# Eight-kilobyte weight runs, and an activation turn moved one step later, in an expert loop on one core

## The reference, cut to what matters

```python
g = jnp.einsum('td,edf->tef', h, p['w_gate'])      # w_gate (64, 1024, 256)
u = jnp.einsum('td,edf->tef', h, p['w_up'])        # w_up   (64, 1024, 256)
a = jax.nn.silu(g) * u * comb[..., None].astype(h.dtype)
routed = jnp.einsum('tef,efd->td', a, p['w_down']) # w_down (64, 256, 1024)
```

## Time and profile before

| | us |
|---|---|
| median of 3 runs | 1307.94 |
| lowest and highest | 1305.64, 1310.03 |
| span of the profiled execution, first to last instruction | 1303.8 |
| PE, DVE, ACT, POOL busy | 1130.0, 391.3, 324.9, 306.5 |
| first gate/up product of an item starts | 567.14 |
| last one starts | 1204.92 |

### The profile page before, as it was taken

How to read it: one execution, slowest core, us unless ns; L and a number is a source line. 1 busy time by engine, 2 the same in 40 slices (tenths; PEclk the granted TensorE clock), 3 DMA queues, 4 the chain that set the end, 5 groups by cost and what they waited for, 6 DMA issues and landing times.

```text
span 1303.8 us, 19553 instructions
## 1 busy us (share of the span) xinstructions
PE 1130.0 (87%) x6570; PEld 656.3 (50%) x6571; DVE 391.3 (30%) x936; ACT 324.9 (25%) x708; POOL 306.5 (24%) x500
## 2 busy tenths in 40 slices
PE   3899999898999897489998698899999889988960
PEld 1676676465666544354554344455554445544630
DVE  2200000284553223622222122222222212222587
ACT  2000100295663111222222222222222212222111
POOL 1000100102222000333333233333333323333123
PEclk9699999998997898689999999999999989999995
DMA  9711321213440005729899999999999999899651
GB/s 320 278 65 65 109 93 65 74 64 130 165 159 1 1 1 186 274 88 351 310 350 372 369 374 369 369 366 314 322 340 363 369 362 371 310 368 329 258 188 72
DMA packets 195436, 304.18 MB, mean 233 GB/s; under 512 B 13206, under 2 KB 146392, under 8 KB 194568
## 3 DMA queue, kind: packets, MB, share of 16 engines
q1 hardware_dynamic: 178488, 268.26, 59.6%
q0 software_dynamic: 16256, 33.08, 7.0%
q10 hardware_dynamic: 656, 2.36, 0.5%
HBM read 290.26 MB, written 33.82 MB: 249 GB/s over the span
## 4 chain that ended last, share of the span: by engine, by line
PE 68%; DMA 12%; DVE 7%; SPq 7%; issue 2%; ACT 2%; POOL 1%; POOLq 0%; DVEq 0%; ACTq 0%
PE bank L924 19%; DMA arena<-in_w_down 10%; PE bank L931 9%; PE bank L616 6%; PE bank L617 6%; SPq L335 4%; PE bank L675 4%; PE bank L862 4%; PE bank L917 3%; PE bank L786 2%; PE bank L601 2%; SPq L338 1%; DVE arena L1622 1%; PE bank L813 1%; PE bank L609 1%
## 5 line engine op out<-in xcount | busy, mean ns | idle before, releaser
L924 PE MATMUL bank<-arena 128*64 128x256 f32 x2880 | 348.1, 397 | 55.4 <-DMA arena<-in_w_down 42.4
L924 PEld LDWEIGHTS bank<-arena 128*64 128x64 f32 x2880 | 211.6, 142 | 166.2 <-issue 79.8
L931 PE MATMUL bank<-arena 128*64 128x512 f32 x728 | 176.3, 605 | 0.6 <-DVE arena L1580 0.6
L1586 DVE TENSOR_TENSOR arena<-arena,bank 128x128 f32<-128x128 f32 x90 | 25.9, 288 | 385.8 <-ACT arena L1195 381.2
L508 POOL DMA_INDIRECT arena<-h_rows,arena x93 | 98.2, 1056 | 82.5 <-issue 49.8
L516 POOL DMA_INDIRECT y_rows<-arena x91 | 93.2, 1024 | 86.2 <-POOL arena L513 80.6
L616 PE MATMUL bank<-arena 128*128 128x288 f32 x320 | 105.6, 412 | 2.2 <-DVE arena L1273 2.2
L617 PE MATMUL bank<-arena 128*128 128x288 f32 x320 | 105.3, 411 | 0.0
L1580 DVE COPY arena<-bank 128x512 f32<-128x512 f32 x91 | 62.9, 692 | 113.3 <-PE bank L931 113.3
L1195 ACT ACTIVATE arena<-bank 128x128 f32<-128x128 f32 x90 | 25.0, 278 | 271.5 <-PE bank L924 271.5
L1198 ACT COPY arena<-bank 128x128 f32<-128x128 f32 x90 | 23.9, 265 | 218.8 <-PE bank L946 218.8
(11 more groups left out here) (266 smaller groups left out, 1110.1 us busy)
## 6 DMA issues: line engine op xcount, KB each, us to landing
arena<-in_w_gate SPq DMA_DIRECT2D x64, 1024.0 KB
arena<-in_w_up SPq DMA_DIRECT2D x64, 1024.0 KB
arena<-in_w_down SPq DMA_DIRECT2D x64, 1024.0 KB
arena<-in_w_ada SPq DMA_DIRECT2D x12, 2048.0 KB, 8.0
arena<-in_w_in SPq DMA_DIRECT2D x6, 2048.0 KB, 10.8
arena<-y_rows SPq DMA_DIRECT2D x2, 3072.0 KB, 14.0
arena<-in_w_out SPq DMA_DIRECT2D x2, 2048.0 KB, 8.4
arena<-y_rows SPq DMA_DIRECT2D x2, 2048.0 KB, 16.2
```

What stands on the lines that cost most here:

```text
L924: last = pe.matmul(bank[0][n * SLOT:n * SLOT + SLOT, 0:2 * P].rearrange("p (g f) -> p g f", f=P), HGT[:, k % 4, k // 4, :], w[:, :, n * P: ...
L931: last = pe.matmul(bank[3][n * SLOT:n * SLOT + SLOT, :], AE[:, f, :], DN[j][:, f, 512 * n:512 * n + 512], start=(f == 0), stop=(f == 1))
```

## The change

Five things change together. The view of w_gate and w_up becomes `(p k) n -> p k n`: partition p gets channels 8p to 8p + 7, which are one run of 8 KB in HBM, and gate and up lie one behind the other in the slot. The tokens are stored in HBM in the matching order of channels, by a strided read in ACT's copies out of PSUM. On PE the turn of the activations moves out of its own item: it is issued in the next item, right behind `gate_up` and ahead of `turn_in`; its wait for `ac_ready` moves to the head of the item, and the waits of `down` get a `pe_mark` of their own. ACT copies AE first in each item and takes SILU after it, with one extra one-column SILU at the head of each pair of items. DVE copies HGT first and multiplies AC after it.

```diff
             def load_wide(e, j):
-                sp.dma_start(GU[j][:, :, 0:FE], w_gate[0, bass.ds(e, 1)].rearrange("e (k p) n -> p (e k) n", p=P)).then_inc(exp_ld[j], 16)
-                sp.dma_start(GU[j][:, :, FE:2 * FE], w_up[0, bass.ds(e, 1)].rearrange("e (k p) n -> p (e k) n", p=P)).then_inc(exp_ld[j], 16)
+                sp.dma_start(GE[j], w_gate[0, bass.ds(e, 1)].rearrange("e (p k) n -> p (e k) n", k=KC)).then_inc(exp_ld[j], 16)
+                sp.dma_start(UE[j], w_up[0, bass.ds(e, 1)].rearrange("e (p k) n -> p (e k) n", k=KC)).then_inc(exp_ld[j], 16)
...
             def gate_up(j):
                 for k in range(KC):
-                    w = GU[j][:, k, :].rearrange("p (g f) -> p g f", f=FE)
+                    w = GUE[j][:, :, k, :]
...
+            def turn_out():
+
+                pe.transpose(bank[2][:, 0:P], AC, IDENT).then_inc(at_done, 1)
+
             def item(i, j, before):
 
                 pe.wait_ge(hgt_ready, i + 1)
+                pe.wait_ge(ac_ready, i + 1)
                 gate_up(j)
+                turn_out()
                 pe.wait_ge(hg_staged, i + 2)
                 pe.sem_inc(pe_mark)
                 turn_in()
                 pe.wait_ge(ae_ready, i + 1)
                 pe.wait_ge(yo_ready, i + 1)
+                pe.sem_inc(pe_mark)
                 down(before)
-                pe.wait_ge(ac_ready, i + 1)
-                pe.sem_inc(pe_mark)
-                pe.transpose(bank[2][:, 0:P], AC, IDENT).then_inc(at_done, 1)
...
             items = pe.value_load(START[0:1, NE:NE + 1], min_val=1, max_val=NI)
+            pe.wait_ge(ac_ready, items + 1)
+            turn_out()
...
-                act.copy(H2S[0:r, t, 0:512], bank[b][0:r, :])
-                act.copy(H2S[0:r, t, 512:D], bank[b + 1][0:r, :]).then_inc(h2_evac, 1)
+                rows = H2S[0:r, t, :].rearrange("p (k q) -> p k q", q=P)
+                act.copy(rows[:, :, 0:64], bank[b][0:r, :].rearrange("p (q k) -> p k q", k=KC))
+                act.copy(rows[:, :, 64:P], bank[b + 1][0:r, :].rearrange("p (q k) -> p k q", k=KC)).then_inc(h2_evac, 1)
...
             with act.Fori(0, pairs) as g:
+
+                act.activation(CT[:, 0, 2:3], CT[:, 0, 3:4], ACT.Silu)
                 for x in range(2):
                     i = g * 2 + x
+                    act.wait_ge(at_done, i + 1)
+                    act.copy(AE.rearrange("p f s -> p (f s)"), bank[2][:, 0:P]).then_inc(ae_ready, 1)
                     act.wait_ge(gu_done, i + 1)
                     act.activation(SI, bank[0][:, 0:P], ACT.Silu).then_inc(silu_done, 1)
-                    act.wait_ge(at_done, i + 1)
-                    act.wait_ge(dn_done, i + 1)
-                    act.copy(AE.rearrange("p f s -> p (f s)"), bank[2][:, 0:P]).then_inc(ae_ready, 1)
                     act.wait_ge(hgt_done, i + 2)
                     stage(i + 2, x, (g + 2) * 16)
...
             with dve.Fori(0, pairs) as g:
                 for x in range(2):
                     i = g * 2 + x
-                    dve.wait_ge(silu_done, i + 1)
-                    dve.tensor_tensor(AC, SI, bank[0][:, P:2 * P], ALU.mult).then_inc(ac_ready, 1)
                     dve.wait_ge(hgt_done, i + 2)
                     dve.tensor_copy(hgt, bank[1][:, :]).then_inc(hgt_ready, 1)
+                    dve.wait_ge(silu_done, i + 1)
+                    dve.wait_ge(at_done, i + 1)
+                    dve.tensor_tensor(AC, SI, bank[0][:, P:2 * P], ALU.mult).then_inc(ac_ready, 1)
                     out_rows(i, x, (g + 1) * 16)
```

More of the change, by code:

```diff
@@ L111, in build @@
         DN = [at(a_att + 4096 + 2048 * i, 2, D) for i in (3, 0, 1, 2)]
+        gu_base = [a_ring + 4096 * i for i in range(3)] + [a_att]
+        GUE = [at(b, 2, KC, FE) for b in gu_base]
+        GE = [w[:, 0, :, :] for w in GUE]
+        UE = [w[:, 1, :, :] for w in GUE]
         WSG, WSD = GU[0], DN[0]
@@ L1178, in _ @@
             act.wait_ge(h2_stored, 16 * NT)
-            act.activation(AE.rearrange("p f s -> p (f s)"), IDENT, ACT.Copy, scale=0.0).then_inc(ae_ready, 1)
+            act.activation(AC, IDENT, ACT.Copy, scale=0.0).then_inc(ac_ready, 1)
             act.wait_ge(start_ready, 1)
@@ L1206, in first_term @@
                 act.activation(acc, acc, ACT.Copy, scale=W6[0:ROWS[t], t, 0:1]).then_inc(yb_first, 1)
+            act.wait_ge(at_done, pairs * 2 + 1)
+            act.copy(AE.rearrange("p f s -> p (f s)"), bank[2][:, 0:P]).then_inc(ae_ready, 1)
             act.wait_ge(hg_staged, pairs * 2 + 2)
```

## The result

The changed kernel takes 1263.46 us (median of 4 runs, 1261.27 to 1268.75), the kernel before 1306.79 in the same comparison. The ratio is 0.967, with a 95% interval of 0.964 to 0.970: 43 us faster. I had predicted 1290 with a range of 1258 to 1308. The direction and the range held; of the gain I had forecast less than half. In every execution here the device time is some 1.8 us above the profiled span, so the 4.1 us that I added to the span were partly the spread of the kernel before.

What follows compares the result with a forecast made beforehand. PE's own steps and weight transfers were taken to bound the loop in turns. 586.7 + 1 + 31.5 + 0 = 619.2 us against 637.8, so 1307.9 - 18.6 = 1289.3, predicted as 1290, range 1258 to 1308.

Steps and rivals of the forecast that it cites:

- rival 1: PE's queue in the expert loop: the queue cost does not appear, 46 to 55 us saved, 1253 to 1262; chance 0.22.
- What bounds the loop: Expert loop: PE's own steps and transfers take turns as limits, 586.7 us of steps and 51 us of transfer stalls.
- Longer runs: Gate and up loads: 8 KB runs move at 418 to 430 GB/s, taking 4.9 us instead of 6.10 per expert.
- Rival 3: Loop transfers: long runs do not raise the rate, stalls stay, +7 us, 1315; chance 0.13 together with a slow new DMA pattern.
- The queue has no slack at a change: PE's instruction queue at a change of expert ends just when PE is free, with 0.15 us showing.
- The turn costs 0.5 us at each of 63 changes, 31.5 us: Moved activation turn: PE's queue gets 0.57 us longer per change of expert, taken as 0.5, in total 31.5 us.
- The second semaphore: PE's queue ahead of down: a further semaphore instruction after the AE wait, costing 0.15 us per change.
- The wait for AC: PE's queue at the item's head: the wait moved there adds 0.15 us at a change of expert.
- Inside an expert +0.05: Steps between items of one expert: down starts 0.38 us later, 0.26 is paid back; 0.05 x 26 = 1 us.
- Remaining stalls 0: Loop transfers after the change: no stalls left with the queue cost, 5 us without it, 15 as far end.
- The gathers come earlier: `stage` and so the gathers come 2 us earlier per item, which was said only to help.
- The signs: Trace marks named beforehand: pure loads about 420 GB/s, loop rate down, w_down waits under 8 us, changes 6.9 to 7.1.

Runs made afterwards that it cites:

- one_read: The changed kernel with one of two PE reads of START dropped at 48 expert changes, reusing the bound just read: 1259.4 us, ratio 0.964 to the kernel before.
- four_marks: The changed kernel with four more semaphore instructions in PE's queue behind the wait for an expert's weights: 1282.7 us, one run.
- turn_only: The changed kernel with 1 KB runs and plain token copies again, keeping the moved turn and new ACT and DVE order: 1303.1 us, ratio 0.998 to before.
- no_mark: The changed kernel without the `pe_mark` semaphore instruction ahead of down: 1267.1 us, ratio 0.971 to the kernel before.

## Why the prediction was wrong

The range held because it reached far towards rival 1, not because the forecast's mechanism was right.

- *What bounds the loop: right.* Two limits taking turns, 586.7 us of PE's own and 51 of stalls; measured 584.9 and 53.
- *Longer runs: right in kind, right in size at first hand.* 4.88 to 5.02 us for gate and up at 418 to 430 GB/s; they moved at 425 alone. The rate in the loop, 415, is a little below. Two readings were loose: the 430 came from reads of which nearly half the packets were 8 KB, not all 16 KB and more, and 344 and 418 mixed two to one give 366 only when their times are added, 369 as written. Rival 3 fell, since the rate rose. With it fell what the Trainium skill's rule (DMA: Bandwidth & Descriptors, Specifications) would make of this case: from 512 B on all runs at full rate. 1 KB runs are not, 353 against 426 GB/s.
- *The queue has no slack at a change: right.* one_read and four_marks show it.
- *The turn costs 0.5 us at each of 63 changes, 31.5 us: this step failed.* Its working was -0.08 + 0.15 + 0.35 + 0.15 = 0.57. The measured change is 6.50 - 6.46 = 0.04. The start was right: the turn began at T = 798.03 and the AE wait passed at 798.7 (T + 0.67 predicted). But down's 16 instructions cost 0, not 0.35; I had taken the pace of gate/up's 64 (0.022 each) for a price of every instruction. The second semaphore cost 0, not 0.15: line 953 carries both waits and the mark in one instruction. The wait for AC cost about 0.1, not 0.15. That leaves -0.08 + 0.1 = 0.02. Over 63 changes this term was worth some 2 us instead of 31.5.
- *Inside an expert +0.05: the sign was wrong, -0.20.* Down starts at T + 0.78, not T + 0.97, since no second semaphore and no row of eight stand ahead of it, and the turn's place at the item's end was worth more: from down's start to the next product it was 2.13 us (with the turn) and is 1.74 (805.31 to 807.05), 0.39 instead of 0.26.
- *Remaining stalls 0: wrong, 17.5.* PE became faster and not slower; for that case I had 5, counted with 425 GB/s, and the loop moved 415. four_marks, with PE as slow as forecast, still had 6.
- *The gathers come earlier, "which only helps": not so for ACT.* stage waited 28.3 us for them instead of 3.4; this cost PE nothing.
- *The signs.* 425 GB/s in the pure loads came as named. In the loop the rate rose instead of falling, waits on w_down fell to 13.8 and not under 8, and two products of 5.36 us were left. Changes at 6.5 were the sign named for rival 1.

The sum with the measured sizes: PE 581.3 + stalls 17.5 = 598.8, against my 619.2. The outcome is rival 1, to which I gave 0.22: its 1253 to 1262 was 1 us too low, by the stalls. Of its two conditions the second held, that the waits cost next to nothing. The first, that the queue is ahead by the whole of down, was not the cause; the queue passes the AE wait only just ahead of down (798.7 and 798.81).

## What to carry to other kernels

Lay weights out so that each partition's part is one run of several KB where a loop is at nine tenths of its DMA engines: here 1 KB to 8 KB raised the saturated rate from 368 to 415 GB/s, and 4 KB already gave 408. Read the instruction queue of the busiest engine at every branch of the loop; price what stands there by rows that have the same surroundings, an instruction behind a wait and not one in a long row. Where transfers and the engine take turns as limits, an edit to one alone pays only in part (turn_only gave nothing), and unrolling to spare a branch can cost far more than the branch when the body no longer stays loaded.

## What the runs showed of the hardware that I had not expected

- 16 PE instructions behind a passed wait add nothing to the 0.151 us from one queue instruction to the next; 64 in a row take 1.45 us.
- One EVENT_SEMAPHORE instruction of PE carries two waits and an increment. One more of them at a change of expert costs 0.14 to 0.15 us; seven inside gate/up's row cost nothing.
- Behind a weight load that carries the wait for AE, the queue went on only when that load did, 0.01 us later in all 90 items of no_mark.
- At eight experts per turn the loop's branch took 7.3 us and PE idled 11.7 to 14.7 us at each turn (13.7 in the one shown), with 8 to 10 blocks of 16 KB loaded between turns; at four experts per turn it took 0.2 us, and no block was loaded again.
- A moving operand with a stride of two float32 elements made 32 matmuls of 256 columns take 3.79 to 3.81 us instead of 3.62. ACT's strided reads of PSUM (every eighth element) cost nothing: 0.57 to 0.59 us per copy, as before.
